# Gate preparation and state turning of an mLSTM layer placed inside its input projection

## What is computed

```
q, k, v, o, gates = split_cols(h @ w_in, (512, 512, 1024, 1024, 32))
gates = 15 * tanh((gates + gate_b) / 15)          # 4 x 8 heads: i fwd, i bwd, f fwd, f bwd
log_f = log_sigmoid(f gates)
# per direction, chunk by chunk:
bcum = cumsum(log_f)
m_t  = maximum(bcum + m, running max of (bcum_t - bcum_i + i_i))
w_intra, w_inter = exp(...) of differences of these; w_end = their last row
h = (w_inter * q c + s v) / maximum(|den|, exp(-m_t))
```

## Time and profile before

| what | us |
|---|---|
| timed runs, median (lowest to highest) | 4570.85 (4568.16 to 4573.29) |
| profiled execution, first to last instruction (its span; the profile gives no other time of it) | 4575.0 |
| layer 1 input projection, steady part | 2943 to 3226 |
| end of the projection's matmuls to the first instructions of the scan | 3226.6 to 3306.0 |
| mLSTM scan on PE | 3306.1 to 3522.4 |

### The profile page before, as it was taken

How to read it: one execution, slowest core, us unless ns; L and a number is a source line. 1 busy time by engine, 2 the same in 40 slices (tenths; PEclk the granted TensorE clock), 3 DMA queues, 4 the chain that set the end, 5 groups by cost and what they waited for, 6 DMA issues and landing times. The chain is left out here.

```text
span 4575.0 us, 85777 instructions
## 1 busy us (share of the span) xinstructions
PE 3925.4 (86%) x34537; PEld 3566.9 (78%) x34537; DVE 2177.4 (48%) x3748; ACT 1019.5 (22%) x1709; POOL 881.1 (19%) x708
## 2 busy tenths in 40 slices
PE   5999888377777788589999999899397789999998
PEld 3999533266666677389999999799275789999998
DVE  2433455443333454647464556400366556556555
ACT  3100243422222343412010001201144122001001
POOL 2222000000000431111222222122023202222221
PEclk8999899698898799799999999999698899999999
DMA  3222476412121221411111111222032111111111
GB/s 137 83 93 88 150 262 239 155 44 58 44 58 36 84 90 42 159 32 40 43 36 47 41 42 32 64 88 79 29 98 84 57 33 37 50 39 37 46 44 64
DMA packets 418842, 341.24 MB, mean 75 GB/s; under 512 B 62340, under 2 KB 398397, under 8 KB 416029
## 3 DMA queue, kind: packets, MB, share of 16 engines
q1 hardware_dynamic: 407137, 268.20, 19.4%
q0 software_dynamic: 10304, 60.98, 3.3%
q10 hardware_dynamic: 1152, 8.39, 0.5%
HBM read 261.01 MB, written 76.48 MB: 74 GB/s over the span
## 5 line engine op out<-in xcount | busy, mean ns | idle before, releaser
L91 POOL TENSOR_TENSOR ffn_w_lower<-ffn_w,ffn_w_upper 128x1024 fp32r<-128x1024 f32 x164 | 393.1, 2397 | 1361.2 <-DVE ffn_w_upper L86 1361.2
L931 DVE SCALAR_TENSOR_TENSOR rstd<-u_tile,ffn_taps,rstd 128x945 f32<-128x945 f32 (+3 forms) x440 | 490.3, 1114 | 85.5 <-ACT rstd L878 71.5
L99 PE MATMUL ffn_ps<-HU,ffn_w_upper 128*128 128x384 f32 x2112 | 482.0, 336 | 28.9 <-DVE ffn_w_lower L91 25.9
L99 PE MATMUL ffn_ps<-HL,ffn_w_upper 128*128 128x384 f32 x2112 | 481.1, 335 | 0.0
L99 PE MATMUL ffn_ps<-HU,ffn_w_lower 128*128 128x384 f32 x2112 | 480.7, 335 | 0.0
L99 PEld LDWEIGHTS ffn_ps<-HU,ffn_w_upper 128*128 128x128 f32 x2112 | 377.4, 189 | 31.6 <-issue 29.0
L99 PEld LDWEIGHTS ffn_ps<-HL,ffn_w_upper 128*128 128x128 f32 x2112 | 378.0, 189 | 0.0
L99 PEld LDWEIGHTS ffn_ps<-HU,ffn_w_lower 128*128 128x128 f32 x2112 | 377.8, 188 | 0.0
L99 PE MATMUL ffn_out_ps<-g_upper,ffn_w_upper 128*128 128x384 f32 x1056 | 355.7, 337 | 22.9 <-DVE g_lower L91 14.4
L99 PE MATMUL ffn_out_ps<-g_lower,ffn_w_upper 128*128 128x384 f32 x1056 | 354.6, 336 | 0.0
L99 PE MATMUL ffn_out_ps<-g_upper,ffn_w_lower 128*128 128x384 f32 x1056 | 354.5, 336 | 0.0
(11 more groups left out here) (460 smaller groups left out, 6352.3 us busy)
## 6 DMA issues: line engine op xcount, KB each, us to landing
ffn_w<-in_ffn_w_in_dram SPq DMA_DIRECT2D x88, 512.0 KB
ada_w<-in_ada_w_dram SPq DMA_DIRECT2D x40, 1024.0 KB, 5.3
rwkv_units<-unit_rows POOLq DMA_DIRECT2D x8, 2304.0 KB, 9.3
un<-rwkv_units SPq DMA_DIRECT2D x36, 512.0 KB, 3.5
z_even<-z_tile POOLq DMA_DIRECT2D x31, 576.0 KB, 3.1
in_w<-in_ab_w_in_dram SPq DMA_DIRECT2D x31, 512.0 KB
gun<-gdn_units SPq DMA_DIRECT2D x72, 192.0 KB, 3.6
z_odd<-z_tile POOLq DMA_DIRECT2D x24, 576.0 KB, 4.8
```

The source lines that it names most:

```text
L91: return eng.tensor_tensor(out.bitcast(F32R), x, up, ALU.subtract)
L99: mm = pe.matmul(o, w(a).bitcast(F32R), r.bitcast(F32R), start=(first and n == 0), stop=(last and n == 2))
L931: dve.scalar_tensor_tensor(out=o, in0=i, scalar=tp[:, t:t + 1], in1=o, op0=ALU.mult, op1=ALU.add).then_inc(s["conv"] if n < NCONV else s[" ...
```

## The change

The gate columns become the projection's third tile (n = 2 of 25), and `mlstm_in_phase` does what four phases did. The three phases between projection and scan are gone. The gate rows no longer go through memory: POOL copies them from SBUF to SBUF into two groups of eight partitions, 0 to 7 for the forward and 32 to 39 for the backward direction, so that one instruction on 40 partitions handles both (where direction or chunk order differs, two instructions remain, one on partitions 0 to 31 and one on 32 to 39). Steps of the gate chain are placed on ACT and DVE behind the work of numbered tiles; the latent state is loaded after the normalisation has ended, into the space of `rstd`, turned on PE behind tile 6 (its `n` part behind tile 8) and copied out by ACT; the gate columns are made by 27 matmuls behind tile 16, and `w_end` is spread by 16 matmuls behind tile 18. The context state is zeroed by POOL at the start. The scan takes a single column of the identity, repeated 128 times, as weights in place of `sel`, over 40 rows. The projection is written out tile by tile; its loops are gone.

```diff
--- before.py
+++ after.py
@@ setup_phase
-                    link(pool.memset(K["sel"][:], 0.0))
-                    link(pool.affine_select(out=K["sel"][:], in_=K["sel"][:], compare_op=ALU.not_equal, fill=1.0,
-                                            base=0, pattern=[[-1, 8], [0, P]], channel_multiplier=1))
...
@@ mlstm_prep_phase is taken out; mlstm_in_phase takes its place and that of mixer_in_phase
+GATE_ROWS = (slice(0, 8), slice(32, 40))
+GR_N = 40
...
+    TAIL = 2
+    N = ML_T + 1
...
+        g = tmp[0:GR_N, 0:2, :]
+        gi, gf = g[:, 0], g[:, 1]
+        en, wi = t0[:], reset[:]
+        cs = K["rstd"][:, 0:2 * 4 * P].rearrange("p (d q x) -> p d q x", d=2, q=4)
...
+                    def load(n):
+                        k = n % 2
+                        if n >= 2:
+                            sp.wait_ge(low[k], n // 2)
+                        sp.dma_start(cols(W, n), w_tail if n == TAIL else w_src[tile_of(n)]).then_inc(w_in[k], 16)
+                    load(0)
+                    load(1)
+                    sp.wait_ge(s["small_zeroed"], 2)
...
+                    for n in range(2, 5):
+                        load(n)
+                    sp.wait_ge(s["n_lower"], 2 * KD)
+                    for d in range(2):
+                        sp.dma_start(cs[:, d].rearrange("v q (h k) -> v (q h) k", h=2),
+                                     c_src[0, 0, d].rearrange("h v k -> v h k")).then_inc(s["stage_in"], 16)
+                        sp.dma_start(ns[:, d, :], n_src[0, 0, d].rearrange("(q h) k -> q (h k)", h=2)).then_inc(s["stage_in"], 16)
+                    for n in range(5, N):
+                        load(n)
...
+                    def tile(n):
+                        k = n % 2
+                        pe.wait_ge(low[k], n // 2 + 1)
+                        pe.wait_ge(z_ok[k], n // 2)
+                        out = ps[0:32, k] if n == TAIL else ps[:, k]
+                        matmul_tile(pe, out, (cols(WU, n), cols(WL, n)), X, KD).then_inc(mm_done[k], 1)
+
+                    def turn_c():
+                        pe.wait_ge(s["stage_in"], 64)
+                        for d, bank in enumerate((pc, pw)):
+                            for q in range(4):
+                                mm = pe.transpose(bank[:, q * P:q * P + P], cs[:, d, q, :], K["ident"][:])
+                        mm.then_inc(s["c_turned"], 1)
...
+                    def gate_cols():
+                        pe.wait_ge(s["rows"], 1)
+                        pe.wait_ge(s["n_copied"], 1)
+                        pick = K["ident"][0:GR_N, 0:64].rearrange("p (d x) -> p d x", d=2)[:, :, 0:8]
+                        for c in range(NCH):
+                            for i, src in enumerate((gi, wi, en)):
+                                o = c * 48 + i * 16
+                                mm = pe.matmul(pc[:, o:o + 16], src[:, c * P:c * P + P], pick, start=True, stop=True)
+                        mm.then_inc(s["cols"], 1)
+
+                    def end_rows():
+                        pe.wait_ge(s["we_ok"], 1)
+                        for q in range(4):
+                            for d in range(2):
+                                for h in range(2):
+                                    r = 32 * d + 2 * q + h
+                                    mm = pe.matmul(pw[HALF[h], (2 * q + d) * NCH:(2 * q + d + 1) * NCH],
+                                                   K["ident"][0:GR_N, r:r + 1].to_broadcast([GR_N, 64]), we[:],
+                                                   start=True, stop=True)
+                        mm.then_inc(s["we_ps"], 1)
...
+                    for n in range(2, N):
+                        tile(n)
+                        if n == 6:
+                            turn_c()
+                        if n == 8:
+                            turn_n()
+                        if n == 16:
+                            gate_cols()
+                        if n == 18:
+                            end_rows()
...
+                    for n in range(N):
+                        tile(n)
+                        if n == 4:
+                            act.wait_ge(s["bias_ok"], 1)
...
+                        if n == 6:
+                            act.wait_ge(s["abs_ready"], 1)
+                            link(act.activation(t0[:], gf, ACT.Abs))
+                            link(act.activation(t0[:], t0[:], ACT.Exp, scale=-1.0))
+                            link(act.activation(t0[:], t0[:], ACT.Ln, bias=1.0))
...
+                        if n == 15:
+                            act.wait_ge(s["rows"], 1)
+                            act.activation(we[:], we[:], ACT.Exp).then_inc(s["we_ok"], 1)
...
+                    def stabilise(n):
+                        for d, r in enumerate(GATE_ROWS):
+                            r = slice(32 * d, r.stop) if d else slice(0, 32)
+                            x, e = chunk(n, d)
+                            sd = -1 if d else 1
+                            a, M = gi[r, x][:, ::sd], MN[r, x][:, ::sd]
+                            link(dve.tensor_tensor_scan(M, a, a, mp[r, n:n + 1], ALU.max, ALU.max))
...
+                    for n in range(3, N):
+                        cut(n)
+                        if n == 7:
+                            dve.wait_ge(s["tanh"], 2)
+                            link(dve.tensor_scalar(g, g, GATE_CAP, None, ALU.mult))
+                            dve.nop().then_inc(s["abs_ready"], 1)
+                        if n == 9:
+                            dve.wait_ge(s["softplus"], 1)
...
+                        if 11 <= n < 14:
+                            for i in range(3 * (n - 11), 3 * (n - 10)):
+                                stabilise(i)
...
+                        if n == TAIL:
+                            pool.wait_ge(s["g_zeroed"], 1)
+                            for i in range(4):
+                                pool.dma_start(g[GATE_ROWS[i % 2], i // 2, :], z[8 * i:8 * i + 8, k, :]).then_inc(s["g_in"], 16)
+                        else:
+                            pool.dma_start(zc[tile_of(n)], z[:, k, :]).then_inc(stored[k], 16)
...
@@ mlstm_scan_phase
-                            c = chunk(it, d)
-                            mm = pe.matmul(ps[:, g, 0, i * P:i * P + P], K["sel"][:, 2 * q + h, :], MN[:, d, c * P:c * P + P],
+                            c, r = chunk(it, d), 32 * d + 2 * q + h
+                            mm = pe.matmul(ps[:, g, 0, i * P:i * P + P], K["ident"][0:GR_N, r:r + 1].to_broadcast([GR_N, P]), MN[:, c * P:c * P + P],
...
@@ trunk_kernel
-                    mixer_in_phase(nc, K, K["gain"][:, 1, 0], shift(1, 0), A["ml_w_in"][0], ML_T, 32, zc2, ztail2, None, ML_O)
...
+                        mlstm_in_phase(nc, A, K, K["gain"][:, 1, 0], shift(1, 0), A["ml_w_in"][0], zc2, mm_out, ml_ctx, ml_lat)
...
-                            mlstm_prep_phase(nc, A, K, ztail2, mm_out)
-                            zero_states_phase(nc, [ml_ctx[:]])
-                            with ExitStack() as t:
-                                turn_states_phase(nc, K, [], odd_states(nc, t, A["state_mlstm_c"], A["state_mlstm_n"], ml_lat))
-                            mlstm_scan_phase(nc, K, zc2, ml_ctx, ml_lat)
...
+                        mlstm_scan_phase(nc, K, zc2, ml_ctx, ml_lat)
```

More of the change, by code:

```diff
@@ new lines, in mlstm_in_phase, with cols, tile_of, stores_before @@
+        w_src = w[:, 0:ML_T * P].rearrange("(k p) (m c) -> m p k c", p=P, c=P)
+        w_tail = w[:, ML_T * P:ML_T * P + 32].rearrange("(k p) c -> p k c", p=P)
+        def cols(t, n):
+            return t[:, n % 2, :, 0:32] if n == TAIL else t[:, n % 2]
+        with phase(nc, "w_in0", "w_in1", "upper0", "upper1", "lower0", "lower1", "mm0", "mm1", "z0", "z1", "stored0", "stored1",
+                   "g_zeroed", "g_in", "small_zeroed", "small_in", "bias_ok", "tanh", "abs_ready", "softplus", "rows", "we_ok",
+                   "cols", "we_ps", "link_d", "link_a", "m_stored", "ctx_m", "stage_in", "c_turned", "c_copied", "n_turned",
+                   "n_copied", "state_zeroed", *NORM_SEMS) as s:
+            norm = Norm(K, s, X, gain, shift, [tmp[:, i] for i in range(4)])
+            w_in, up, low, mm_done, z_ok, stored = [
+                [s[n + "0"], s[n + "1"]] for n in ("w_in", "upper", "lower", "mm", "z", "stored")]
+            def tile_of(n):
+                return n if n < TAIL else n - 1
+            def stores_before(n):
+                return sum(1 for i in range(n) if i % 2 == n % 2 and i != TAIL)
@@ L2936, in _ @@
-                    dve.wait_ge(s["tanh"], 4)
-                    link(dve.tensor_scalar(g[:], g[:], GATE_CAP, None, ALU.mult))
-                    dve.nop().then_inc(s["abs_ready"], 1)
-                    dve.wait_ge(s["sp"], 1)
-                    link(dve.scalar_tensor_tensor(out=g[:, 2:4], in0=g[:, 2:4], scalar=0.0, in1=t0[:], op0=ALU.min,
-                                                  op1=ALU.subtract))
-                    for d in range(2):
```

(12 more changed lines are left out.)

236 lines of the change are left out of this document (145 added, 91 removed).

## The result

The changed kernel took 4507.55 us (median of 4 timed runs, 4500.58 to 4510.50), the kernel before 4569.51 us beside it (4562.10 to 4573.29). The ratio is 0.986, with a 95% interval of 0.9846 to 0.9874: 62 us less, 58 to 70 by the interval. The profiled execution's span went from 4575.0 to 4508.2 us, 66.8 less.

What follows compares the result with a forecast made beforehand. PE bounds the input projection; a serial chain fills the gap behind it. Gap 79.4, less phase's end 9.3, less PE insertions 15.9, plus 0.4, gives 54.6 us less: 4516 us, range 4503 to 4535.

Steps and rivals of the forecast that it cites:

- The gap: Serial chain between the projection's last gate sums and the scan's first DMA: all of its 79.42 us goes.
- The phase's end: Last tile's copy, store, landing and restart before the scan: 9.3 us remain of the gap, between 7.6 and 10.2.
- Gate columns: 27 small matmuls on PE in the projection: 9.1 us with the clock falling midway, 11.1 with the slow start behind.
- the slow tile: Projection tile behind the gate columns starts at half clock: 1.5 to 2.6 us lost, 2 taken.
- Spreading of `w_end`: 16 matmuls on PE in the projection: 2.4 us, plus 1 for a possible clock fall, 3.4 us.
- Turning: 8 transposes of 128 columns and 2 small ones on PE in the projection: 1.4 us, 2.8 at half clock.
- Other engines at nothing: Work added on DVE, ACT, POOL and SP in the projection fits inside their waits and costs nothing.
- The third tile: Its weights in the projection are a quarter in size, so PE's wait there goes: 0.4 us less.
- The scan at nothing: The scan's own work is the same in number and size and starts at half clock in both: no change.
- first rival: Clock holds through the projection's small matmuls: PE's part is 10.1 us, the time 4510; chance 0.22.
- Rivals 2 and 4: 2: something in the projection stalls, 4521 to 4535, chance 0.15. 4: a late wait keeps the chain, up to 4566, 0.04.

Runs made afterwards that it cites:

- The SyncE version: The changed kernel with the projection's last store issued by SyncE's queue instead of GpSimd's: 4511.88 us.
- The version with three of the 27: The changed kernel with only the first 3 of the 27 gate-column matmuls, the other 24 left out: 4497.70 us.

## Why the prediction was right, and where it was not

**The gap** was read rightly: it was one chain, and all that could be moved gained its whole length.

**The phase's end** was put at 9.3 us and took 7.95. From the store's issue to the next transfer it took 6.5 us, against 4.8 + 3.06 from the earlier trace rows: the store landed in 3.0 us and the restart took 3.5. I had added a median landing from one place to a restart read at another; the shortest landing, 3.1, would have given 7.6. The SyncE version shows that the queue of the last store is itself a term, 2.9 us, most of it in the restart.

**Gate columns**, forecast 11.1, measured 11.09. The split within it held as well: 0.111 us a record for 0.117, 0.213 for 0.234, a fall (about 3 us in, a little earlier than forecast), and 2.1 us for the slow tile where I took 2. This is the step on which forecast and first rival (4510, clock held) parted, and the rival is refuted by the clock of 0.53 from 3131 to 3142, though its number, 4510, lay nearer to 4507.55 than the forecast: that is the scan's doing, and says nothing for the rival. The version with three of the 27 prices the fall at 4.7 us.

**Spreading of `w_end`**, forecast 3.4, measured 1.24. This term was mis-sized. I took 0.074 us a record from a row with 129 moving columns; with 9 moving columns a record took about 0.03. Whether the shorter moving side is the cause no run shows. And I put 1 us on a fall of the clock that did not come.

**Turning**, forecast 1.4, measured 1.28, with no slow start behind it. By the rule that I quoted from the Trainium skill (TensorE: Matmul & The Clock Gate, Part 4: PE-mode transpose) it would have left one, 2 us more. In the traces the matmuls behind the eight transposes are at once back at their usual length, so the row decided rightly; they lasted 0.8 us, though, and a longer run of them between large matmuls was not tried.

**Other engines at nothing**: right, PE has no idle time in the projection behind 2943. The third tile gave back 0.6 where I took 0.4.

**The scan at nothing**: wrong, and the largest error, 8.4 us in the profiled executions. By the experiments 5.8 to 6.9 us of it are the rows; the rest is open. The step that failed is the sentence that the scan's own work is the same in number and size. It is, in instructions and columns, and its weight loads did take the 0.187 us that I looked at; but its spreading matmuls read 40 rows where they read 8, and I never looked at the scan's granted clock, which stood at 0.92 with PE busy for 94% of the time and so had something to give. I had allowed a few microseconds for a clock that falls at other places, in the range and not in the sum. Of the 12.2 us between the span expected (4520.4) and found (4508.2), 8.4 lie in the scan, 2.4 in the projection, 1.4 in the phase's end. In medians the miss is only 8.5 us (4516 against 4507.55), because the median lay 4.15 us below the profiled span before and 0.65 after; that this nearly cancels the 3.8 us outside of the scan is luck. So is part of the hit: the time is below all that the terms allow (4509), and inside the range only by the margin set below them.

**Rivals 2 and 4** did not come about: no stall, and no wait for the rows behind tile 16. Rival 2's own upper end does not follow from its terms: 4516 and 15 us are 4531, not 4535.

## What to carry to other kernels

A stretch that PE bounds at a clock below 1.00 is not fixed: look at which small matmuls run ahead of each fall, and whether a padded operand (here 40 rows for 8, with zeros; a record takes 272 ns, median, where it took 270) keeps it up. A change that reshapes an operand for another reason, here to hold both directions in one tile, can move the clock of every phase that reads it, so its rows belong in the sum. Cut the traces at events that both kernels have and compare stretches: where the work was the same they repeated here to tenths of a microsecond, while the whole time moved by ten.

## What was not expected of the hardware

- Matmuls with 8 rows in the scan let the clock fall with PE busy (0.92, 0.90, 0.90 in the 66 us from the scan's 18th microsecond), those with 40 or 128 rows held it at 1.00 there in nine of eleven executions and at 0.97 in two, also with zeros in the added rows.
- A stationary operand read as one column repeated 128 times loads as fast as a stored tile: a median of 187 ns with 40 rows, and of 185 with 8 rows where the stored one takes 187. With 8 rows the ratio for the whole kernel is 0.9998 (0.9984 to 1.0012).
- 2.1 us of matmuls with 16 columns, between large ones, were followed by a fall in two of three places; 0.7 us of them, 0.8 us of transposes and 1.0 us of the `w_end` spreading were not.
- A pause of 2.24 us behind 6 us of full-size filling work left PE at half clock (eight spreading matmul records in 2.04 us); with one of 1.28 us, behind 4 us of it, they took 1.13 us. Each was seen in one execution.
